# Input norm split between ScalarE and VectorE, low-rank products of w and a side by side, and fill steps and marks moved in a hybrid-mixer kernel

## What is computed

```
for l in range(2):
    h = rmsnorm(x, norm_g[l])
    p = h @ w_in[l]                       # 1024 x 8904 columns, split among the mixers and gates
    oa = band_attention(...)  * silu(az)  # A
    ob = hgrn2(...)           * silu(bz)  # B: gated linear recurrence, chunks of 64
    oc = top_k_attention(...) * silu(cz)  # C: indexer, 256 keys chosen per query
    od = rwkv7(...)           * silu(dz)  # D: w and a from low-rank codes wd, ad
    x = x + (sum_i sigmoid(g_i) * (o_i @ w_branch[l, i])) @ w_out[l]
out = rmsnorm(x, final_g)
```

## Time and profile before

| | |
|---|---|
| median of three runs | 3019.27 us |
| the profiled execution | 3018.58 us |
| its span, first to last instruction | 3016.8 us |
| TensorE busy | 2883.6 us, 96% |
| VectorE, ScalarE, GpSimd busy | 1560.9, 970.7, 813.8 us |
| mean granted TensorE clock | 0.993 |

### The profile page before, as it was taken

The page is one execution under the profiler, slowest core; times in us unless marked ns, Lnnn a source line. Parts: engine busy times, 40 slices in busy tenths (PEclk is TensorE's granted clock), DMA queues, the critical chain, the costliest instruction groups (busy, mean ns, idle before and its releaser), DMA issues. The chain is left out here.

```text
span 3016.8 us, 46711 instructions
## 1 busy us (share of the span) xinstructions
PE 2883.6 (96%) x18888; PEld 1541.7 (51%) x18888; DVE 1560.9 (52%) x3173; ACT 970.7 (32%) x1836; POOL 813.8 (27%) x572
## 2 busy tenths in 40 slices
PE   7998999999999999999999989999999999999998
PEld 3446454575544465444445464545755444654443
DVE  2587867533358812155226878674333598030643
ACT  2255663211133324300113556632111333253001
POOL 2026412312133232232020353133021332322320
PEclk9999999999999999999999999999999999999999
DMA  5001101101121221263040011011010212212631
GB/s 213 18 28 37 42 24 44 51 16 40 33 76 39 77 85 65 91 212 112 0 140 18 29 42 42 20 51 43 16 43 34 81 33 93 80 46 94 228 100 56
DMA packets 132493, 195.80 MB, mean 65 GB/s; under 512 B 8088, under 2 KB 88120, under 8 KB 132024
## 3 DMA queue, kind: packets, MB, share of 16 engines
q1 hardware_dynamic: 113688, 158.74, 16.3%
q10 hardware_dynamic: 18592, 34.09, 3.0%
HBM read 146.14 MB, written 48.78 MB: 65 GB/s over the span
## 5 line engine op out<-in xcount | busy, mean ns | idle before, releaser
L509 PE MATMUL ps<-hT,wr 128*128 128x512 f32 x1600 | 748.8, 603 | 0.5 <-issue 0.5
L509 PEld LDWEIGHTS ps<-hT,wr 128*128 128x128 f32 x1600 | 289.8, 191 | 306.2 <-issue 298.0
L509 PE MATMUL ps<-sums,wr 128*128 128x512 f32 x800 | 383.0, 607 | 4.5 <-ACT gts L579 4.5
L660 POOL TENSOR_TENSOR gts<-gts,wr 128x512 f32<-128x512 f32 x96 | 134.9, 1406 | 633.5 <-ACT wr L560 484.2
L509 PEld LDWEIGHTS ps<-sums,wr 128*128 128x128 f32 x800 | 145.4, 193 | 155.0 <-issue 145.1
L738 PE MATMUL ps<-xo,arena 128*128 128x512 f32 x512 | 220.1, 592 | 0.0
L635 POOL TENSOR_TENSOR wr<-wr 128x512 f32<-128x512 f32 (+1 forms) x56 | 87.2, 1558 | 450.6 <-PE ps L509 320.7
L1137 DVE CUSTOM_DVE_ANT_0 arena<-ps,arena 128x640 f32<-128x640 f32 (+7 forms) x128 | 90.4, 706 | 213.8 <-PE ps L1038 196.0
L509 PE MATMUL ps<-wr 128*128 128x512 f32 x400 | 191.6, 602 | 6.5 <-ACT wr L560 6.5
L1507 DVE TENSOR_SCALAR_CACHE_REDUCE arena<-arena,sm 128x384 f32<-128x384 uint16 (+7 forms) x256 | 192.8, 810 | 2.2
L560 ACT ACTIVATE wr<-ps 128x512 f32<-128x512 f32 x150 | 89.1, 594 | 303.5 <-PE ps L509 289.3
(11 more groups left out here) (316 smaller groups left out, 4714.5 us busy)
## 6 DMA issues: line engine op xcount, KB each, us to landing
wr<-in_w_in SPq DMA_DIRECT2D x68, 1024.0 KB, 5.4
gate_tanh<-gts ACTq DMA_DIRECT2D x128, 256.0 KB, 2.1
arena<-gate_tanh SPq DMA_DIRECT2D x128, 256.0 KB, 3.0
x_cur<-arena SPq DMA_DIRECT2D x2, 4096.0 KB, 24.3
arena<-in_w_branch SPq DMA_DIRECT2D x8, 1024.0 KB, 9.8
wr<-in_w_out SPq DMA_DIRECT2D x8, 1024.0 KB, 6.9
arena<-x_cur SPq DMA_DIRECT2D x4, 2048.0 KB, 8.8
arena<-in_x SPq DMA_DIRECT2D x4, 1024.0 KB, 8.3
```

What stands on the lines that cost most here:

```text
L509: ins = pe.matmul(ap, lhsT=right(u, w_side)[:, kt, :], rhs=left(h_side, kt), start=fresh and kt == 0, stop=kt == half_k - 1, skip_group_ch ...
L660: pool.tensor_tensor(dst, dst, stage_of(u), ALU.add).then_inc(sg("pool_added"), 1)
```

## The change

The input norm of layer 0 gets functions of its own. For each half of the rows, ScalarE squares the first two tiles and VectorE the other two (`tensor_tensor_reduce`); mean, root and reciprocal are made once for four tiles; then each engine scales its two tiles. The load of the identity is issued from ScalarE. In D, w and a are computed for the same piece together, a pair of products in T and O, with one fill step after each pair. Fill steps: before C's attention 70 becomes 59; D start 6 becomes 2, D kk 19 becomes 21; B start three times 16 becomes four times 12; "end" 3+3 becomes 4+4 in the first half; "khn" 2 becomes 3 in the first half; "adds" (3, 3, 3, 11, 3) becomes (3, 3, 3, 13, 1), of which the first half of B uses four. ScalarE empties jobs at one more place between its Ln instructions and at a new mark in the middle of B's turn.

```diff
-TOPK_FILL = 70
+TOPK_FILL = 59
...
-D_FILL = {"start": 6, "kk": 19, "bonus": 37, "decay": 10, "CH": 2, "Y": 1, "X": 2, "UZ": 1, "P": 1, "S": 1, "norm": 12, "turn": 24}
-B_FILL = {"start": 16, "end": 6, "khn": 2, "adds": (3, 3, 3, 11, 3), "att": 1, "last": 2, "turn": 8}
+D_FILL = {"start": 2, "low": 1, "kk": 21, "bonus": 37, "decay": 10, "CH": 2, "Y": 1, "X": 2, "UZ": 1, "P": 1, "S": 1, "norm": 12, "turn": 24}
+B_FILL = {"start": 12, "end": (8, 6), "khn": (3, 2), "adds": (3, 3, 3, 13, 1), "att": 1, "last": 2, "turn": 8}
...
-                        pe.wait_ge(sg("rows_normed"), 4 * half + 4)
+                        pe.wait_ge(sg(f"rows_normed{half}"), 4)
...
+            def act_norm_first(act):
+
+                for part in range(2):
+                    act.wait_ge(sg(f"x_in{2 * part}"), 16)
+                    if part:
+                        act.wait_ge(sg("squares_first"), 2)
+                    for n in range(2):
+                        r = 4 * part + n
+                        act.activation(H(16 + n), xin[:, r, :], ACT.Square, accum_out=ssq[:, r:r + 1]).then_inc(sg("squares_first"), 1)
+                    c = slice(4 * part, 4 * part + 4)
+                    act.wait_ge(sg("mean_square_first"), part + 1)
+                    act.activation(root[:, c], msq[:, c], ACT.Sqrt).then_inc(sg("root_first"), 1)
+                    act.wait_ge(sg("inverse_first"), part + 1)
+                    for n in range(2):
+                        r = 4 * part + n
+                        act.activation(xo[:, r, :], xin[:, r, :], ACT.Copy, scale=inv[:, r:r + 1]).then_inc(sg(f"rows_normed{part}"), 1)
+
+            def dve_norm_first(dve):
+
+                for part in range(2):
+                    dve.wait_ge(sg(f"x_in{2 * part + 1}"), 16)
+                    for n in range(2):
+                        r = 4 * part + 2 + n
+                        ins = dve.tensor_tensor_reduce(out=H(18 + n), in0=xin[:, r, :], in1=xin[:, r, :], scale=1.0, scalar=0.0,
+                                                       op0=ALU.mult, op1=ALU.add, accum_out=ssq[:, r:r + 1])
+                    link(dve, ins)
+                    c = slice(4 * part, 4 * part + 4)
+                    dve.wait_ge(sg("squares_first"), 2 * part + 2)
+                    dve.tensor_scalar(msq[:, c], ssq[:, c], 1.0 / D, EPS, ALU.mult, ALU.add).then_inc(sg("mean_square_first"), 1)
+                    dve.wait_ge(sg("root_first"), part + 1)
+                    dve.reciprocal(inv[:, c], root[:, c]).then_inc(sg("inverse_first"), 1)
+                    dve.wait_ge(sg("inverse_first"), part + 1)
+                    for n in range(2):
+                        r = 4 * part + 2 + n
+                        dve.tensor_scalar(xo[:, r, :], xin[:, r, :], inv[:, r:r + 1], None, ALU.mult).then_inc(sg(f"rows_normed{part}"), 1)
...
-                    for n in range(3):
+                    for n in range(4):
                         pe_fill(pe, B_FILL["start"])
                         jobs.mark(("B start", n))
                     for m in range(2):
-                        pe_fill(pe, B_FILL["end"] // 2)
+                        pe_fill(pe, B_FILL["end"][m] // 2)
                         jobs.mark(("B end", m, 0))
-                        pe_fill(pe, B_FILL["end"] // 2)
+                        pe_fill(pe, B_FILL["end"][m] // 2)
...
-                        pe_fill(pe, B_FILL["khn"])
+                        pe_fill(pe, B_FILL["khn"][m])
...
-                    pe_fill(pe, B_FILL["turn"])
+                    pe_fill(pe, B_FILL["turn"] // 2)
+                    jobs.mark("B turn")
+                    pe_fill(pe, B_FILL["turn"] // 2)
                     pe_fill_unit(pe)
...
                     act.activation(two, bc_flat, ACT.Ln, bias=1.0)
+                    act_fills(act, ("B start", 1))
...
-                    act_fills(act, ("B start", 2))
+                    act_fills(act, ("B start", 3))
...
+                    act_fills(act, "B turn")
                     act.wait_ge(sg("b_square"), 1)
...
-                    for what, r0 in (("w", 0), ("a", 64)):
-                        for m in range(2):
-                            for half in range(2):
-                                key = ("D" + what, m, half)
-                                ap = jobs.open(pe, key, [T, O][half])
+                    for m in range(2):
+                        for half in range(2):
+                            aps = [jobs.open(pe, ("D" + what, m, half), bk) for what, bk in (("w", T), ("a", O))]
+                            for what, r0, ap in (("w", 0, aps[0]), ("a", 64, aps[1])):
                                 jobs.filled(pe.matmul(ap, lhsT=Pr("up", P * m, P * m + P)[r0:r0 + 64, :],
-                                                      rhs=wd[r0:r0 + 64, 512 * half:512 * half + 512], start=True, stop=True), key)
+                                                      rhs=wd[r0:r0 + 64, 512 * half:512 * half + 512], start=True, stop=True),
+                                            ("D" + what, m, half))
+                            pe_fill(pe, D_FILL["low"])
...
-                    for n, (what, buf) in enumerate((("w", lw), ("a", a))):
-                        for m in range(2):
-                            for half in range(2):
+                    for m in range(2):
+                        for half in range(2):
+                            for n, (what, buf) in enumerate((("w", lw), ("a", a))):
...
+                        act.dma_start(con[:, 0:P], consts[:, 0:P]).then_inc(sg("ident_loaded"), 16)
...
-                        sp.dma_start(con[:, 0:P], consts[:, 0:P]).then_inc(sg("ident_loaded"), 16)
```

More of the change, by code:

```diff
@@ L933, in dve_norm @@
                         else:
-                            dve.tensor_scalar(xo[:, row, :], xin[:, row, :], inv[:, c], None, ALU.mult).then_inc(sg("rows_normed"), 1)
+                            dve.tensor_scalar(xo[:, row, :], xin[:, row, :], inv[:, c], None, ALU.mult)
+            def act_norm_first(act):
[13 more added lines that the diff above has]
+                        act.activation(xo[:, r, :], xin[:, r, :], ACT.Copy, scale=inv[:, r:r + 1]).then_inc(sg(f"rows_normed{part}"), 1)
@@ L2061, in dve @@
                     dve.tensor_tensor(tmp, kk, kk, ALU.mult).then_inc(sg("kk_square"), 1)
-                    for half in range(2):
-                        jobs.stored(dve, ("Da", 1, half))
+                    for what in "wa":
+                        jobs.stored(dve, ("D" + what, 1, 1))
                     dve.tensor_scalar(lw, lw, 1.0, -0.5 * EXPM5, ALU.add, ALU.mult)
@@ L2218, in _ @@
                     if l == 0:
+                        act.dma_start(con[:, 0:P], consts[:, 0:P]).then_inc(sg("ident_loaded"), 16)
                         act.wait_ge(sg("root_table"), 1)
                         act.activation(root, msq, ACT.Sqrt)
-                        act_norm(act, "first", sg("rows_in"), range(NT))
+                        act_norm_first(act)
                         act.wait_ge(sg("par_loaded"), 16)
@@ L2232, in _ @@
                     if l == 0:
-                        def rows_step(i):
-                            dve.wait_ge(sg(f"x_in{i // 2}"), 16)
-                            dve.engine_nop().then_inc(sg("rows_in"), 1)
                         dve.memset(msq, 1.0).then_inc(sg("root_table"), 1)
-                        dve_norm(dve, "first", rows_step, range(NT))
+                        dve.wait_ge(sg("root_table"), 1)
+                        dve_norm_first(dve)
                         dve.wait_ge(sg("con_loaded"), 16)
```

## The result

The kernel after takes 3046.82 us (median of 4 runs, 3045.11 to 3048.22), the kernel before beside it 3019.86 (3017.55 to 3020.47): ratio 1.0090, 95% interval 1.0073 to 1.0108. The forecast of 3021.0 was wrong, and 3046.8 lies 20 us above its range.

What follows compares the result with a forecast made beforehand. TensorE's work plus its idle time was taken as the bound. Layer 0 at -0.7, layer 1 at +1.7 and startup at +0.7 gave +1.7 us, so 3021.0 from 3019.27; range 3013.5 to 3027 us.

Steps and rivals of the forecast that it cites:

- Unit of account: All fill work: eight matmul records are four fill steps and take 3.44 us, so a step is 0.86 us.
- startup: Layer 0's input norm: the first projection starts at about 24.9 us against 24.24, +0.7 us once (-0.5 to +1.3).
- C's search: Before C's attention: search ends 1.4 us earlier, TensorE idles about 8.4 us, -1.4 us per layer, 11 steps owed.
- D's start: D's low-rank stage: 3.4 us idle, paired products, 9.5 us stage; next product ends -0.4 us (layer 0), +0.3 (layer 1).
- the first part: Fill-step count: 4 fewer before B's turn, which then holds 21 instead of 17; from there nothing differs.
- the third rival: B's waits stay because GpSimd's additions move with the fill phase: +2.1 us per layer, 3025 us, chance 0.10.
- B: B before its turn: four TensorE waits, 4.9 us, go and five steps come: -0.6 us per layer (-1.0 to +1.5).
- B's turn: End of B: the 2.26 us wait goes, 21 steps take 18.0 us: -0.9 us in layer 0, +0.8 in layer 1.
- The clock: Behind C's gap it surely halves, +1.5 us per layer (0 to 3.4); at D's start it may, +1.1 (0 to 2.0).
- the gap is dear: C's first tiles and D's start: half clock lasts longer, +2.8 us per layer, some 3027 us, chance 0.18.
- the gaps are free: C and D: clock doesn't fall or its cost hides in waits, C's attention gains: 3012.6 us, chance 0.17.
- the pairs don't run side by side: D's low-rank stage: a cycle takes 2.6 us, not 2.5: +0.3 us per layer, 3021.6 us, chance 0.03.

Runs made afterwards that it cites:

- e12: The input norm's part of the change alone on the kernel before: 3018.83 us, ratio 1.0001.
- e8: The kernel after with GpSimd's weight sums cut to 8 columns from the fourth unit on: 3019.48 us, ratio 1.0008.
- e5: The kernel before with 89 fill steps beside C's search instead of 70: 3042.0 us, ratio 1.0082.
- e9: The kernel after with 87 fill steps beside C's search instead of 59: 3021.65 us, ratio 1.0010.
- e3: B's part of the change alone on the kernel before: 3018.24 us, ratio 0.9995.
- e17: The kernel after with 64 fill steps beside C's search instead of 59: 3019.73 us, ratio 1.0005.
- e16: The kernel after with 92 fill steps beside C's search instead of 59: 3000.90 us, ratio 0.9941.
- e7: The kernel before with GpSimd's weight sums cut to 8 columns from the fourth unit on: 2998.0 us, ratio 0.9933.
- e13: The kernel after with 70 fill steps beside C's search and GpSimd's weight sums left out from the fourth unit on: 3004.0 us, ratio 0.9953.
- e2: The kernel before with 59 fill steps beside C's search instead of 70, nothing else changed: 3059.39 us, ratio 1.0133.

## Why the prediction was wrong

By its own steps, layer 0 unless said:

- **Unit of account and startup**: right. 0.9 for 0.7 us; the cost doesn't last (e12).
- **C's search, the gap, D's start**: right in mechanism, 0.9 us short from the first projection to the bonus product. TensorE idles 8.09 us for 8.4 (9.4 less 1.4, of the forecast's own numbers, is 8.0), and its clock halves in both layers and again just after D's start (0.51 from 480 to 483 us). The pairs run side by side; a cycle takes 2.54 us at full clock for a forecast 2.5, whose four terms add up to 2.4. All this was worth +9.2 in the measure above, and 10.3 came.
- **The step that failed** is the one that ends D's part: "VectorE's later chain waits for TensorE's bonus product anyway and moves with it". It does move with TensorE, but GpSimd doesn't. GpSimd's weight sums move with the fill work, and that had fallen back by 9 steps against D, 7.7 us. Before, three sums at D's end (from 864.10) fell mostly beside a reduce and a small operation; after, they came to lie on the two-input operations: 10.2 us in layer 0 and 9.0 in layer 1. Leaving the sums out takes this loss away (e8); the phase alone, without a gap, brings 8.0 of it (e5) and 7.9 (e9); with 92 steps the change loses 0.4 us there.
- Behind it stands a wrong sentence of the first part: that the 4 steps owed are paid in the turn "and from there on nothing differs". True from the turn on, and it hid what the owed steps do until then. I had the collision in view for B only, as the third rival, with 2.1 us a layer and a chance of 0.10.
- **B**: from D's turn to B's states 3.0 us were won for 4.9 forecast (two small waits are new). e3, with the phase of before, has the forecast's gain: 5.4 us.
- **B's turn**: right in layer 0, 4.6 us won for 4.3. In layer 1 0.6 us were lost between B's states and the turn where 2.6 were to be won. In B's value stage TensorE stood idle there for 2.34 us up to 2553.94, for which the profile names no other engine, and then ran at half clock (two fill records take 1.65 us at 2557.67, 1.13 elsewhere). e9, with the same steps, has no such idle time.
- **The clock** behind the gaps: the forecast took it as near certain at 8 us, from the earlier trace rows. The Trainium skill, "TensorE: Matmul & The Clock Gate", section "HAM oscillation — how this bites in real kernels", on which the prediction also drew, says that a long enough wait makes the next work start cold, and the trace agrees. The clock fell in both layers, behind 8.09 us, and behind 5.19 in e17.
- **The rival "the gap is dear"** priced the clock alone, 2.8 us a layer. The gap cost 12.6 us a layer against e9. Two thirds of that are its idle time, which the forecast did count (+8.8 at C's first turn) and let the owed steps win back in the waits of D, B and the turn. Behind D's turn they did: 7.6 us of 9.2. But these waits go without a gap too (e9 wins 7.2 us there), so the gap is never free: it only hides a gain. Without it and in the better phase the same edits reach B's turn at -8.1 (e16). The rivals "the gaps are free" and "the pairs don't run side by side" fell: the clock did fall, and the pairs do run side by side.

The size of what was missed, in layer 0: forecast 0.0 at B's turn, found +12.9 = 0.2 (startup) - 0.4 (to C's turn) + 1.3 (to the bonus product) + 10.2 (D) + 1.9 (B) - 0.3 (turn). D's term was put at nothing, and it is four fifths of the miss.

What stays open: why the gap's price grows from 10.0 us at the bonus product (after against e9) to 12.3 at D's turn in the same phase, and what would become of the kernel if GpSimd's sums were kept off VectorE altogether; e7 and e13 bound that by leaving them out. Whether 92 is the best number was not tried either. And D's collision alone doesn't explain the time with the sums left out: e8 still stands 21.5 us above e7.

## What to carry to other kernels

When filler work is moved, list what hangs on its progress on the other engines, and look where that work will land, all the way to the point where the schedules meet again: an engine that is idle for 72% of the time cost 10 us a layer here, through its neighbour. And count idle time of the engine that sets the time as lost unless a wait can be named that the moved work will fill, and that no other part of the same change fills. After a change of this kind, tune the number that sets the phase again: here one constant, from 59 to 92, made 46 us.

## What the runs showed of the hardware

- Beside GpSimd's two-input operations, VectorE's with two SBUF inputs go from 2.29 to 3.24 us at 2048 columns, and GpSimd's of 512 columns from 1.27 to 3.3: they end in turn, as if each waited out the other. A VectorE operation that reads PSUM keeps its 0.41 us, and a reduce of 2048 columns its 2.29.
- The clock can fall with hardly any idle time. In e2 TensorE idled for 0.55 and 0.59 us at D's start and then ran its 64-row products, one after the other, mostly at half clock; why the clock fell there is open. The timeline, and the busy time by stretch with a clock of 0.50 for 12 us:

```profile
477.77 1.98 PE L1821 MATMUL ps<-arena,par 64*128 64x512 f32 x4 [0.55 <-ACT arena L1992]
```

```profile
482.00:494.00 12.00, 12.00 (x15) 4.06 (x14) 11.72 (x13) 3.89 (x6) 0.00 (x0) 0.50 0.00 0
```

Twelve records took 9.35 us there, where the kernel before runs sixteen in 7.68 us.
